# First attention of a two-block model on one core: negated copy of the scores with their minimum, exponential in place from SBUF

## The reference

```
s = einsum('bqhcd,bkhcd->bhcqk', q, k)              # two score maps per head
p = softmax(s / sqrt(64), axis=-1)                  # over the 768 keys
a = p[:, :, 0] - lam * p[:, :, 1]                   # difference of the two maps
o = einsum('bhqk,bkhe->bqhe', a, v)                 # 128 value columns per head
```

## Time and profile before

| | |
|---|---|
| median of 3 runs | 3219.08 us |
| profiled execution, its own time | 3211.04 us |
| its span, from first to last instruction | 3208.9 us |
| first attention, first score product to end of the last transposition | 160.3 us of the span |
| TensorE busy over the span | 3009.8 us (94%) |
| VectorE busy over the span | 1419.1 us (44%) |
| ScalarE busy over the span | 902.6 us (28%) |
| mean granted TensorE clock | 0.971 of full |

### The profile page before, as it was taken

The page is one execution under the profiler, slowest core; times in us unless marked ns, Lnnn a source line. Parts: engine busy times, 40 slices in busy tenths (PEclk is TensorE's granted clock), DMA queues, the critical chain, the costliest instruction groups (busy, mean ns, idle before and its releaser), DMA issues. The chain is left out here.

```text
span 3208.9 us, 38033 instructions
## 1 busy us (share of the span) xinstructions
PE 3009.8 (94%) x15018; PEld 2318.0 (72%) x15018; DVE 1419.1 (44%) x2210; ACT 902.6 (28%) x1422; POOL 274.2 (9%) x290
## 2 busy tenths in 40 slices
PE   6999999899988999999999999999999988989995
PEld 4888888777733677888888887888878765764442
DVE  3646463545566465564333343333332267521112
ACT  3211121232255222223222232222233255321111
POOL 1000000001100100001000011000010155012221
PEclk9999999999989899999999999999999989989998
DMA  5323333221000165453222212223232200438895
GB/s 230 131 97 120 106 114 126 70 85 53 27 1 1 66 240 219 164 211 110 92 93 104 80 51 74 97 83 105 84 112 92 111 27 1 165 125 339 357 369 203
DMA packets 78061, 395.79 MB, mean 123 GB/s; under 512 B 17520, under 2 KB 19952, under 8 KB 51312
## 3 DMA queue, kind: packets, MB, share of 16 engines
q1 hardware_dynamic: 66416, 385.65, 32.6%
q0 software_dynamic: 11520, 8.43, 0.8%
HBM read 444.34 MB, written 16.78 MB: 144 GB/s over the span
## 5 line engine op out<-in xcount | busy, mean ns | idle before, releaser
L676 PE MATMUL ps<-h_high_ffn,weights_high_ffn 128*128 128x512 f32 (+1 forms) x1696 | 624.3, 368 | 8.3 <-DVE weights_low_ffn L811 4.1
L677 PE MATMUL ps<-h_low_ffn,weights_high_ffn 128*128 128x512 f32 (+1 forms) x1696 | 623.5, 368 | 0.0
L678 PE MATMUL ps<-h_high_ffn,weights_low_ffn 128*128 128x512 f32 (+1 forms) x1696 | 623.2, 367 | 0.0
L676 PEld LDWEIGHTS ps<-h_high_ffn,weights_high_ffn 128*128 128x128 f32 x1696 | 320.2, 189 | 63.7 <-issue 9.5
L678 PEld LDWEIGHTS ps<-h_high_ffn,weights_low_ffn 128*128 128x128 f32 x1696 | 320.1, 189 | 52.9
L677 PEld LDWEIGHTS ps<-h_low_ffn,weights_high_ffn 128*128 128x128 f32 x1696 | 320.3, 189 | 52.5
L676 PE MATMUL ps<-hidden_high_ffn,weights_high_ffn 128*128 128x512 f32 (+1 forms) x880 | 328.1, 373 | 17.7 <-DVE weights_low_ffn L811 10.4
L760 ACT ACTIVATE weights_high_ffn<-weights 128x2048 fp32r<-128x2048 f32 (+4 forms) x160 | 244.0, 1525 | 346.2 <-PE ps L678 275.5
L811 DVE TENSOR_TENSOR weights_low_ffn<-weights,weights_high_ffn 128x2048 fp32r<-128x2048 f32 (+4 forms) x160 | 289.6, 1810 | 84.2 <-ACT weights_high_ffn L760 82.7
L677 PE MATMUL ps<-hidden_low_ffn,weights_high_ffn 128*128 128x512 f32 (+1 forms) x880 | 326.6, 371 | 0.0
L678 PE MATMUL ps<-hidden_high_ffn,weights_low_ffn 128*128 128x512 f32 (+1 forms) x880 | 326.4, 371 | 0.0
(11 more groups left out here) (439 smaller groups left out, 4578.3 us busy)
## 6 DMA issues: line engine op xcount, KB each, us to landing
weights<-in_ffn_gu SPq DMA_DIRECT2D x88, 1024.0 KB, 4.9
big<-in_w_exp_gu SPq DMA_DIRECT2D x32, 2048.0 KB, 9.4
scratch_ffn<-in_w_mod SPq DMA_DIRECT2D x35, 1536.0 KB, 6.6
weights<-in_ffn_d SPq DMA_DIRECT2D x24, 768.0 KB, 4.2
weights<-in_w_in SPq DMA_DIRECT2D x16, 1024.0 KB, 4.8
weights<-in_ffn_d SPq DMA_DIRECT2D x24, 640.0 KB, 3.9
weights<-in_w_exp_dn SPq DMA_DIRECT2D x15, 1024.0 KB
hbuf<-in_w_exp_dn SPq DMA_DIRECT2D x12, 1024.0 KB
```

The costliest lines, as they stand in the source:

```text
L676: pe.matmul(out, wh, xh, start=(k == 0), stop=False)
L677: pe.matmul(out, wh, xl, start=False, stop=False)
L678: mm = pe.matmul(out, wl, xh, start=False, stop=(k == n - 1))
```

## The change

VectorE's pass over each score map no longer takes only the maximum. It adds zero (a column of `column` that is 0, spread over the row), multiplies by -1, writes the result to `pr[u % 2][:, c]` in SBUF and keeps the minimum in `top`, which is again the negated maximum. ScalarE's exponential reads that SBUF copy, with scale -1, and writes it in place. The scores of the next tile wait for the two passes instead of the two exponentials. In VectorE's list the passes for tile `u + 1` stand ahead of the tail of tile `u`. The wait on the transpositions of tile `u - 2` moves from ScalarE to VectorE.

```diff
@@ -1329,7 +1329,7 @@
                 def scores(u):
                     hd, q = u // QT, u % QT
                     if u > 0:
-                        pe.wait_ge(fm["exp"].sem, 2 * u)
+                        pe.wait_ge(fm["top"].sem, 2 * u)
@@ -1441,11 +1441,9 @@
                 for u in range(tiles):
-                    if u >= 2:
-                        scalar.wait_ge(fm["turned"].sem, u - 1)
                     for c in range(2):
                         scalar.wait_ge(fm["top"].sem, 2 * u + c + 1)
-                        scalar.activation(pr[u % 2][:, c, :], sc[:, c, 0:NT], ACT.Exp, bias=top[:, u % 2, c:c + 1],
+                        scalar.activation(pr[u % 2][:, c, :], pr[u % 2][:, c, :], ACT.Exp, bias=top[:, u % 2, c:c + 1], scale=-1.0,
                                           accum_out=total[:, c, u:u + 1]).then_inc(fm["exp"].sem, 1)
@@ -1491,14 +1489,21 @@
                 vector.memset(column[:, HEADS - 1:HEADS], 1.0).then_inc(fm["column"].sem, 1)
-                for u in range(tiles):
+
+                def negated(u):
                     for c in range(2):
                         vector.wait_ge(fm["scores"].sem, 2 * u + c + 1)
-
                         if u >= 2:
                             vector.wait_ge(fm["exp"].sem, 2 * (u - 2) + c + 1)
-                        vector.reduce_max(top[:, u % 2, c:c + 1], sc[:, c, 0:NT], AX_X, negate=True)\
-                            .then_inc(fm["top"].sem, 1)
+                            vector.wait_ge(fm["turned"].sem, u - 1)
+                        vector.tensor_tensor_reduce(pr[u % 2][:, c, :], sc[:, c, 0:NT], column[:, 0:1].to_broadcast([P, NT]), -1.0, 3e38,
+                                                    ALU.add, ALU.min, top[:, u % 2, c:c + 1]).then_inc(fm["top"].sem, 1)
+
+                vector.wait_ge(fm["column"].sem, 2)
+                negated(0)
+                for u in range(tiles):
+                    if u + 1 < tiles:
+                        negated(u + 1)
                     if u >= QT and u % QT == 3:
                         output(u // QT - 1)
                     vector.wait_ge(fm["exp"].sem, 2 * u + 2)
```

## The result

| | before | after |
|---|---|---|
| median of the runs | 3218.66 us (4 runs, 3214.24 to 3228.68) | 3333.53 us (4 runs, 3320.39 to 3344.73) |
| profiled execution, its own time | 3211.04 us | 3344.73 us |
| its span | 3208.9 us | 3342.6 us |
| first attention in it | 160.3 us | 279.8 us |
| the rest of the span | 3048.6 us | 3062.8 us |

A forecast was written before the change was run, and what follows sets the result against it. A ring of waits, not a full engine, bounds the first attention. The new ring's 238.8 us plus 55.3 for the clock, less 160.3, gives plus 133.8 on 3219.1: 3353 us, range 3320 to 3389.

The forecast's parts named there:

- the new ring: First attention: scores, copies, tail, transpositions, values, sums, next scores run one after another; 7.75 us per tile with values.
- The wait forecast before the transpositions: TensorE idles before transpositions, waiting for VectorE's difference: about 3.6 us each, near 110 us in all.
- The cover that was named: TensorE's wait on VectorE and ScalarE, which hid transpositions, values and sums before; claimed gone after the change.
- The pieces: Full-clock tile: scores 1.60 us, tail (reciprocal to difference) 1.47, transpositions to values 0.72, values 1.81, sums 0.95.
- The copies: VectorE's two passes per tile: 1.00 us each, 2.00 a pair, bounds 1.82 and 2.54, plus 0.10 to the reciprocal.
- The clock: TensorE in the attention: half its ring work at 1.2 GHz, adding 55.3 us; mean granted clock near 0.75.
- The sum: Attention 238.8 plus 55.3 us, 294.1 against 160.3: plus 133.8 us, putting the median at 3353 us.
- The full clock: Rival: same ring, under a quarter of the work at low clock; plus 78.5 us, 3298 us; chance 0.09.
- The low clock throughout: Rival: over three quarters of TensorE's ring work at the low level; 3409 us; chance 0.13.
- The faster case: Rival: early bank release lets everything overlap, VectorE bounds; attention 125 us, 35 us faster, 3184 us; chance 0.04.
- The other condition named: VectorE's tail ahead of the copies, an alternative order needed for the 125 us attention, 35 us faster; chance 0.04.
- Free terms: No cost: ScalarE's SBUF reads, 2.6 us in all, and VectorE's low part of output weights, 2.3 us.

The follow-up runs named there:

- order_alone: Kernel before with only VectorE's maxima for tile u+1 moved ahead of its tail for tile u: 3326.76 us, ratio 1.0350 to before.
- copy_old_order: Changed kernel with VectorE's old order (copies of a tile, its tail, then the next copies), early score release kept: 3207.24 us, ratio 0.9984 to before.
- ahead2: Changed kernel with TensorE issuing scores(u+2) ahead of the transpositions of tile u, VectorE's new order kept: 3226.13 us, ratio 1.0006 to before.
- values_first: Changed kernel with a tile's values' product and sums moved ahead of its transpositions in TensorE's list: 3262.83 us, ratio 1.0137 to before.
- fill: Changed kernel with 11 useless identity products per tile where TensorE waits for the difference: 3288.16 us, ratio 1.0229 to before.
- changed_again: The changed kernel, unaltered, run once more beside others on one chip: 3336.88 us, ratio 1.0342 to before.
- ahead3: Changed kernel with scores issued two tiles ahead and a third buffer for copied scores and probabilities: 3203.69 us, ratio 0.9929 to before.
- copy_old_release: Changed kernel with VectorE's old order and scores again waiting for the exponentials: 3218.27 us, ratio 1.0009 to before.

## Why the prediction was right, point by point

- **What bounds the kernel, and the new ring.** Right, and shown from four sides: the order alone makes the loss (order_alone), the order undone removes it (copy_old_order), scores moved ahead in the other queue remove it too (ahead2), and work taken out of the ring shortens a tile at the full clock by nearly its own length (values_first). The wait forecast before the transpositions, 3.6 us each and near 110 in all, is 3.31 in the tile shown and 108.5 in all. The cover that was named, the wait beside which turn, values and sums used to run, was gone.
- **The pieces.** Scores 1.60 us forecast, 1.59 found; tail 1.47 and 1.47; turn, values and sums 0.72, 1.81, 0.95 and 0.71, 1.81, 0.96.
- **The copies.** Forecast 2.00 us for a pair and 0.10 to the tail, a term that no row had shown; found 1.76 and none. Lines of the kernel after:

```profile
L1499 DVE CUSTOM_DVE_ANT_0 first_prob<-ps,column x64: 951/956/959, 875.8 to 1142.6; 128x768 f32<-128x768 f32 x64
L1499 DVE DVE_READ_ACCUMULATOR2_ANT top<- x64: 82/83/85, 876.6 to 1143.5; 128x1 f32 x64
```

  One copy takes the 0.95 us worked out from the earlier trace rows, but the next starts 0.88 us after it (993.58, 994.46), and the reads of the accumulator and the reciprocal start inside the end of the one before. The 1.27 us between two passes of 1024 elements was scaled down too little, and the lower end was badly chosen: 1.82 is how long a pair of maxima is busy, not how far apart two starts are. This is the mis-sized term: 32 x (2.10 - 1.76) = 10.9 us. With it the sum at the full clock is 238.8 - 10.9 = 227.9, and fill measured 230.3; a tile with values takes 7.40 us in fill, for 7.75.
- **The clock.** Forecast: half of TensorE's ring work at the low level, 55.3 us. Found: 279.8 - 227.9 = 51.9 us in the profile of after, 274.9 - 227.9 = 47.0 in the second, and 44.6 to 49.5 against fill. The mean was 0.76 and 0.79 where 0.75 was forecast. The size is right in part by luck. The prediction took every tile to be half low, after a stretch whose mean of 0.75 then itself fell to 0.60. In the trace the low level is not spread evenly: the scores of the first six tiles take 2.55 to 2.93 us, and from the tenth tile on it comes back once in each head, behind the tile that has no values' product, as here:

```profile
975.18 1.56 PE L1336 MATMUL ps<-K,Q 64*128 64x512 f32 x8
...
980.65 0.94 PE L1346 MATMUL ps<-ident,first_prob 128*128 128x128 f32 x6 [3.91 <-DVE first_prob L1516]
...
981.53 2.93 PE L1336 MATMUL ps<-K,Q 64*128 64x512 f32 x8
```

  TensorE waited 3.91 us, did six transpositions, and the next scores took 2.93 us instead of 1.56; the scores of the three tiles behind them are mostly back at 1.56. The same six places are low in changed_again (2.75 to 2.93). Also, 3.8 us of work in a tile of 7.75 does not fit the prediction's own pieces (7.75 - 3.57 = 4.18); it enters no sum.
- **The sum.** Plus 133.8 us was forecast, plus 119.5 found in the attention and plus 115 at the medians, 3333.5 us for 3353. The profiled execution's own plus 133.7 matches the forecast by chance, since 14.2 of it lie outside the first attention.
- **The rivals.** The full clock: 78.5 us over before was its price; fill, which makes it true, has plus 73, and plus 70 in the attention. The low clock throughout did not come: tiles at the full clock, like the one in the timeline above, stand among slower ones. The Trainium skill, TensorE: Matmul & The Clock Gate, section "HAM oscillation", says that bursts between waits begin at the low level again and again. The runs agree in part: the mean of 0.76 to 0.79 lies halfway, and the low level begins anew once a head, not in every tile. The faster case's condition was named rightly (scores(u+2) ahead of turn(u)), but its price was not: at that condition alone (ahead2) the time is that of before, because the copies then wait for the buffer that the transpositions read, a wait that stood in the diff. With the third buffer (ahead3) it gave 18.8 us, where 35 had been written. The other condition named, the tail ahead of the copies (copy_old_order), gave 5 to 8 us: an attention of 151.3, not 125.
- **Free terms.** The exponential from SBUF took 927 ns instead of the earlier trace rows's 897, and copy_old_release shows that together with the copies it costs nothing that can be measured. The low part of the output weights was free, as said: it ran from 899.20 for 2.28 us, while VectorE's next copy (903.37) was still waiting for its scores.

## What to carry to other kernels

With hand-ordered queues, write the ring out before and after a reordering: an instruction moved ahead on one engine delays everything behind it, and if that is what another engine's queue stands on, two queues that used to overlap begin to take turns. Work ahead on the producer's side (scores two tiles ahead) and buffers to match belong to the same edit as work ahead on the consumer's side; work ahead on the consumer's side alone lost 112 to 115 us, both sides without a third buffer gave nothing, with it 19 us were won. Work ahead on the producer's side alone was not run. And where TensorE's idle time grows, add what the clock will take: here it was 45 to 50 us on top of 70.

## What the runs showed of the hardware

Useless products can pay. In fill TensorE executes 11 more products a tile, in a wait that it has anyway, and the kernel is 42 to 45 us faster. The granted clock in the attention goes from 0.76 to 0.99, and the real products, which are on the ring, take little more than half the time where they had been at 1.2 GHz (592 against 1062 ns for a values' product). They are written to a part of a PSUM bank that the transpositions leave free, and wait for the evacuation of the tile before; no run shows whether that wait is needed. A pass that copies 768 elements from PSUM to SBUF and keeps their minimum has the pace of the plain maximum over them: 0.88 us from start to start, where a pair of maxima is busy for 1.82 us, which is 0.95 and 0.87.
